# The transfers of a modulation matrix move from GpSimd's queue to ScalarE's queue, in groups of four

## What is computed

```
def adaln(cond, mod_w, mod_b):
    return jnp.split(jax.nn.silu(cond) @ mod_w + mod_b, 6, axis=-1)
```

## Time and profile before

| | before |
|---|---|
| median of three executions | 3646.84 us |
| the profiled execution | 3652.07 us |
| its span, first to last instruction | 3650.3 us |
| TensorE busy | 3305.8 us, 91% |
| mean granted TensorE clock | 0.947 |
| modulation tiles | 96 of 512 KB |

### The profile page before, as it was taken

One profiled execution on the slowest core, in us unless ns is written; L12 is line 12 of the kernel. 1 busy time (PEld: TensorE's weight loads), 2 busy tenths in 40 slices (PEclk: granted clock), 3 DMA queues, 4 the chain that ended last, 5 costly groups with the idle time before them and its releaser, 6 DMA issues.

```text
span 3650.3 us, 67685 instructions
## 1 busy us (share of the span) xinstructions
PE 3305.8 (91%) x25680; PEld 2864.8 (78%) x25680; DVE 2307.3 (63%) x4542; ACT 1387.8 (38%) x2128; POOL 380.0 (10%) x232
## 2 busy tenths in 40 slices
PE   7889899999998979889999999696779998899798
PEld 6678898989886859888999988473558877695798
DVE  5549786868975548976777895447632234636444
ACT  4334334343444333434344344323422223424343
POOL 1137500000000216810000000000000000000000
PEclk9789999999999979999999999897889999899899
DMA  7544445454454733445455445120012322211253
GB/s 252 173 138 141 143 136 188 148 188 148 151 172 161 271 127 126 151 142 177 156 171 168 147 154 190 35 76 1 1 57 93 98 97 90 79 53 47 93 183 124
DMA packets 131695, 478.62 MB, mean 131 GB/s; under 512 B 14512, under 2 KB 16560, under 8 KB 130992
## 3 DMA queue, kind: packets, MB, share of 16 engines
q1 hardware_dynamic: 115696, 416.72, 34.6%
q0 software_dynamic: 15808, 59.25, 4.8%
HBM read 474.87 MB, written 1.05 MB: 130 GB/s over the span
## 4 chain that ended last, share of the span: by engine, by line
PE 77%; DVE 18%; ACT 2%; issue 2%; DMA 1%; POOL 0%; SPq 0%; ACTq 0%; DVEq 0%
PE bank L448 76%; DVE arena L1478 1%; DVE arena L1677 1%; DVE arena L1475 1%; DVE arena L1522 1%; DVE arena L1474 1%; DVE arena L1477 1%; DVE arena L1501 1%; DVE arena L1476 1%; DVE Wl L1296 1%; DVE arena L1519 1%; PE bank L725 1%; DMA HA<-mods 1%; ACT Wh L911 1%; DVE arena L1664 1%
## 5 line engine op out<-in xcount | busy, mean ns | idle before, releaser
L448 PE MATMUL bank<-HR,Wh 128*128 128x256 f32 (+1 forms) x8192 | 1283.6, 310 | 142.1 <-DVE HR L1672 60.0
L1296 DVE TENSOR_TENSOR Wl<-ring,Wh 128x1024 fp32r<-128x1024 f32 x676 | 826.8, 1224 | 924.5 <-ACT Wh L911 923.4
L448 PEld LDWEIGHTS bank<-HR,Wh 128*128 128x128 f32 x8192 | 1137.9, 195 | 223.3 <-issue 69.1
L911 ACT CAST Wh<-ring 128x1024 fp32r<-128x1024 f32 x788 | 824.4, 1046 | 718.3 <-PE bank L448 715.1
L448 PE MATMUL bank<-Wh,HR 128*128 128x512 f32 (+1 forms) x3072 | 688.3, 354 | 2.7 <-DVE HR L1582 2.7
L448 PE MATMUL bank<-HR,Wl 128*128 128x256 f32 (+1 forms) x4096 | 659.0, 304 | 13.8 <-DVE Wl L1296 7.5
L448 PEld LDWEIGHTS bank<-HR,Wl 128*128 128x128 f32 x4096 | 577.0, 193 | 44.8 <-DVE Wl L1296 7.9
L448 PEld LDWEIGHTS bank<-Wh,HR 128*128 128x128 f32 x3072 | 535.1, 189 | 84.1 <-issue 4.2
L448 PE MATMUL bank<-Wl,HR 128*128 128x512 f32 (+1 forms) x1536 | 414.5, 351 | 0.0
L448 PE MATMUL bank<-arena 128*128 128x32 bf16 (+4 forms) x6624 | 342.4, 199 | 49.5 <-DVE arena L1566 11.3
L448 PEld LDWEIGHTS bank<-arena 128*128 128x128 bf16 (+3 forms) x6624 | 243.9, 105 | 109.6 <-issue 55.4
(11 more groups left out here) (224 smaller groups left out, 1931.0 us busy)
## 6 DMA issues: line engine op xcount, KB each, us to landing
ring<-weights SPq DMA_DIRECT2D x788, 512.0 KB, 3.3
HA<-mods POOLq DMA_DIRECT2D x96, 512.0 KB, 6.6
arena<-bias POOLq DMA_DIRECT2D x16, 256.0 KB, 2.9
arena<-keys POOLq DMA_DIRECT2D x2, 1024.0 KB, 5.4
HA<-mla POOLq DMA_DIRECT2D x1, 1536.0 KB, 6.5
K<-constants SPq DMA_DIRECT2D x1, 1402.0 KB, 6.4
X<-x SPq DMA_DIRECT2D x1, 1024.0 KB, 9.0
X<-context POOLq DMA_DIRECT2D x1, 1024.0 KB, 6.6
```

The costliest lines, as they stand in the source:

```text
L448: return nc.tensor.matmul(out, lhsT, rhs, start=first, stop=last)
L911: nc.scalar.copy(Wh[:, i % SPL], ring[:, i % RAW]).then_inc(S("hi_done"), 1)
L1296: v.tensor_tensor(Wl[:, i % SPL], ring[:, i % RAW], Wh[:, i % SPL], ALU.subtract).then_inc(S("lo_done"), 1)
```

## The change

POOL issues no modulation tile any more. ACT does, in groups of four: a function `mod_load(l, b)` issues the four tiles of one block. The first group stands ahead of the first norm of layer 0. The group of block b + 1 stands inside `mod_evac(l, b)`, behind its wait for the four products of block b and ahead of the copy. The first group of layer 1 stands behind ACT's two copies of the accumulator at the end of layer 0.

```diff
+            def mod_load(l, b):
+
+                for n in range(4 * (MODB * l + b), 4 * (MODB * l + b + 1)):
+                    act.dma_start(mslot[n % MSLOT], mod_d[n].rearrange("p (a b) -> p a b", a=4)).then_inc(S(f"mod_in{n % MSLOT}"), 16)
+
             def mod_evac(l, b):
 
                 act.wait_ge(S("mod_mm"), 4 * (MODB * l + b + 1))
+                if b + 1 < MODB:
+                    mod_load(l, b + 1)
                 after(act, S("mod_tp"), MODB * l + b - 1)
                 nc.scalar.copy(mstage[b % 2], macc(b)[:, :].rearrange("p (a b) -> p a b", a=2)).then_inc(S("mod_ev"), 1)
 
             for _i in range(2):
                 nc.scalar.copy(col[:, 90 + _i:91 + _i], eps[:, :]).then_inc(S("h_ev"), 1)
+            act.wait_ge(S("x_in"), 16)
+            mod_load(0, 0)
             for l in range(L):
...
                     nc.scalar.copy(acc[:, half, 0, :], bank[4 + half][:, :]).then_inc(S("acc_first"), 1)
+                if l + 1 < L:
+                    mod_load(l + 1, 0)
             norm_act("fin", X[:, :, XS], T, [(S("peer_out"), L)])
...
-            pool.wait_ge(S("const_in"), 16)
-            pool.wait_ge(S("x_in"), 16)
             for l in range(L):
-                after(pool, S("acc_done"), l)
-                for j in range(4 * MODB):
-                    n = 4 * MODB * l + j
-                    after(pool, S("mod_mm"), n - MSLOT + 1)
-                    pool.dma_start(mslot[n % MSLOT], mod_d[n].rearrange("p (a b) -> p a b", a=4)).then_inc(S(f"mod_in{n % MSLOT}"), 16)
                 pool.wait_ge(S("h_out"), SPLITS[f"m{l}"][1])
```

## The result

The changed kernel takes 3749.01 us (median of four runs, 3748.03 to 3750.19) against 3647.01 us (four runs, 3646.60 to 3647.25), a ratio of 1.028 with a 95% interval of 1.0262 to 1.0298. That is 102 us slower. The forecast was 3665 us with a range up to 3685.

What follows compares the result with a forecast made beforehand. PE was taken to bound the kernel, with 77% of the chain. Start 2.6, blocks 2 to 5 8.4, block 7 1.4 and head loop 6.1 summed to +18.5 us on 3646.84, 3665 us, range 3649 to 3685.

Steps and rivals of the forecast that it cites:

- H = 2.6 us: On ACT: issuing a group of four tiles holds everything behind it for 2.6 us, with ends 1.3 and 4.4.
- Start, +2.6: Ahead of layer 0's first norm square: the first group's whole hold is on the path, +2.6 us.
- Blocks 2 to 5, +4.2: In the projections: groups leave some 4.3 us later and tiles land late, +4.2 us per layer, +8.4 in two.
- the high end: Blocks 2 to 5: one ring tile ahead of each group's last, 1.4 us more each, together 6.5 us per layer.
- The middle, 4.2: Blocks 2 to 5: 4.2 us per layer, taken between the low end 1.8 and the high end 6.5.
- Cost nothing: Projections: ACT's late casts and evacuations have three tiles of lead, about 8.6 us of PE work, so cost nothing.
- Rival C: Blocks 2 to 5: new waits drop PE's clock, about 2.6 us more behind each block, eight times; 3686 us, chance 0.12.
- Block 7, +0.7: Behind block 7: the copy is held 2.6 us, less 1.9 gained on tile waits, +0.7 us per layer.
- Head loop, +3.1: Copies of blocks 8 and 9: holds delay head copies by 1.1 and 1.95 us, +3.1 per layer.
- Free parts: Block 10's copy and layer 1's first group: ACT's idle 5.9 and 2.94 us cover the holds; block 11 issues none.
- Rivals A: Whole kernel: issues are cheap but loads are still late, +4.6 us, 3651 us, chance 0.17.
- Rival B: Block 7: faster landing on the hardware queue removes all 10.3 us of waiting, about 3637 us, chance 0.06.

Runs made afterwards that it cites:

- run 4: The kernel before, POOL's transfers, with ACT held about 2.6 us by 11 tiny copies wherever the changed kernel issues a group ahead of a copy, and at the start: 3668.92 us.
- run 8: The kernel before, with block 6 multiplied behind the second of the last four projection tiles and copied behind the third's evacuation: 3648.40 us, ratio 1.0.
- Runs 1: The changed kernel, with ACT issuing block 5's group right behind block 4's products, one projection tile earlier: 3702.53 us, 1.0171 of before.
- run 2: The kernel before, POOL's queue, with only block 5's group delayed to about where the changed kernel issues it: 3701.72 us, 1.0149 of before.
- run 3: The changed kernel, with 16 unused matmuls of 512 columns ahead of the last four projection tiles: 3741.93 us, 1.0257 of before.
- run 6: The kernel before, POOL's queue, with the groups of blocks 2 to 5 delayed to about the changed kernel's moment: 3740.77 us, 1.0258 of before.
- run 5: The changed kernel, with ACT issuing the groups of blocks 2 to 5 right behind the products of the block in front: 3675.21 us, 1.0092 of before.
- run 7: The changed kernel, with groups 2 to 5 early, other groups behind their copies and the first behind the first square: 3663.51 us, 1.008 of before.
- run 9: The kernel before, POOL's queue, block 5's group late, and PE doing block 5 behind projection tile 14, not 15: 3677.09 us, 1.0065 of before.

## Why the prediction was wrong

The sign was right, the size was not: +18.5 forecast, +102 measured. The profiled executions differ by 96 us (3748.03 against 3652.07). Layer 0 can be laid beside the steps; layer 1's first square comes at 1198.18 instead of 1150.56, 47.6 us later in all.

- **H = 2.6 us, right.** Four issues take 2.59 us. The value was reached by a queue that takes in two and stalls; the trace shows 0.55 for the first and about 0.67 for each other, so the working was not what happens, only its sum. Nor was x worked off when the issue behind it ended at 3.80 us: the page of before has x landed 9.0 us behind its issue at 1.20. The Trainium skill's "usually small" (DMA: Bandwidth & Descriptors, "Issuing engines are not separate DMA queues") agrees with 0.65 us for an issue against 6.5 us to landing; what it costs depends on what waits behind it, and the holds alone cost 20 us in run 4.
- **Start, +2.6, right in size by luck.** The square starts 1.4 us later, not 2.6, since the issues begin beside the last cast; the first norm's sums then took 6.61 us for 5.42, and block 0 is 2.6 us late.
- **Blocks 2 to 5, +4.2, the first step that failed.** They end 18.9 us late, 16.3 behind the start's 2.6. The term's step was "the fourth lands 7.5 us behind the first issue". In the changed kernel the fourth landed 10.7, 11.4, 10.8 and 12.2 us behind it in these blocks. Below, block 5's group before (issues at 90.8 to 93.1) and after (108.8 to 110.8):

```profile
L1834 POOL DMA_DIRECT2D HA<-mods x4: 751/751/751, 90.8 to 93.1; - x4
...
DMA to landing us min/median/max: 3.9/6.3/8.8
```
```profile
L929 ACTq DMA_DIRECT2D HA<-mods x4: 547/652/653, 108.8 to 110.8; - x4
...
DMA to landing us min/median/max: 5.3/7.2/10.3
```

  The first fence is the kernel before, and this could have been read there: the last landed 11.0 us behind the first issue, and in blocks 2 to 4 it was 11.5, 12.7 and 11.2. Landing did not get slower; the time allowed for it shrank. POOL's groups had left 10.5 to 13.1 us ahead of their block, and PE takes the fourth some 1.5 us into it, so all but block 3's (0.70 us) were in time; ACT's left 6.3, 6.3, 8.1 and 6.4 us ahead. Even the high end, with one weight tile in between and so 8.9 us, was low for every group. By the prediction's own terms, two weight tiles in between give 3.3 + 5 x 1.4 = 10.3 us, an estimate that leaves 0.4 to 1.9 us open. The middle, 4.2, is shown by no run: the weight tile issued at 63.69, behind all four of block 2's group, landed at 70.67, ahead of the group's last at 71.69. The waits make 10.3 of the 16.3; the other 6 are products at half clock, in the blocks and behind them, and the 0.64 us that 8 products take behind a wait for 0.48 in a run of 32.
- **"Cost nothing" behind block 5, the step that broke the forecast.** The four tiles behind it were given no term, and with the turn they cost 20.4 us in each layer, 41 in all. The clock was in the prediction as Rival C, at a chance of 0.12 and for one tile behind each block, and "stretches between blocks run at 0.50" was among its own signs of being wrong. Rival C's condition, waits of 1 to 2 us, came true, and its place in three of the four blocks; its price of 2.6 us per block did not. Behind blocks 2 and 3 stand 256-column tiles, and the clock was back within the first of them, which took 4.5 and 4.4 us for 3.0. Behind block 5 stand the only four of 128 columns, and there it stayed down until they ended. The row of 43 us was not to be seen before; that those tiles differ in shape was. The Trainium skill (TensorE: Matmul & The Clock Gate, "The HAM clock gate") says the clock follows how busy PE has been, and gives sustained work as what brings it up. No run agrees for this stretch: PE was busy for 42.7 us of 42.7 at 0.50.
- **Block 7, +0.7, low.** The stretch from block 6's start to the sums of the attention grew by 3.3 us. The hold ahead of block 7's copy is there as described, 2.6 us. Block 6 ran at half clock, 3.41 us for 1.93. And the gain of 1.9 came out at 0.8 (10.5 us from block 6's end to block 7's, for 11.2): PE waited for tiles only 0.96 us where it had waited 5.14, but 3.35 us for block 6's copy, held by the same issues, where it had waited 0.70, and the group's last tile landed 9.3 us behind the first issue, not 7.5.
- **Head loop, +3.1, near.** From those sums to the end of the head loop it is 4.4 us. At block 9 PE waits 2.64 us for the copy L1016 where it had waited 0.57, 2.1 more for the 1.95 worked out. ACT's copies at L1016 (L1007 before) stand behind the groups as said:

```profile
221.60 2.78 ACTq L929 DMA_DIRECT2D HA<-mods  x4
224.42 0.59 ACT L937 COPY X<-bank 128x512 f32<-128x512 f32 x1 [4.14 <-issue]
224.90 0.48 ACT L1016 COPY arena<-bank 128x384 f32<-128x384 f32 x1
```

- **Free parts, right.** The idle time ahead of the first square of layer 1 is still 2.94 us, and the cast behind block 10 still had 5.64 us of idleness ahead of it.
- **Rivals A and B fell**: A with H, B by the landing time, 6.5 us for a tile and 10.7 to 12.2 for a group; run 8 adds that its prize would not have been paid in full. In Rival B's sum, 5H - 1.3 at H = 0.3 is 0.2 us and not 0.3, which changes nothing.

In layer 0 the steps read 2.6, 16.3, 20.4, 3.3 and 4.4, together 47.0 us. Runs 1, 2 and 3 show the clock as the cause of the largest one, runs 4 and 6 the shares of hold and lateness. The sign was right by the holds and the later issue, both in the forecast; that a loss of this size was missed is down to the landing time and the clock. What stays open is the rest of a group's landing time, and what makes the clock fall in one block and not in another. That each 4 KB row travels in 1 KB packets on ACT's queue was seen, but POOL's groups took as long, so it is not shown to matter.

## What to carry to other kernels

A transfer that leaves as soon as its slot is free should not be tied to a point in another engine's program, however near that point seems. Read from the trace of before how long a whole group takes to land and how far ahead of its use it leaves: here 11.0 to 12.7 us against 10.5 to 13.1, so 4 to 6 us of delay was more than the slack. Price a new wait on TensorE not by its length but by what runs behind it: here some 4 us of waits ahead of a long stretch of 128-column products cost 20 us more. And on an engine that others wait for, put issues behind the instruction they wait for, not ahead of it; from run 5 to run 7 that, with the first group behind its square, gave 12 us.

## What the runs showed of the hardware

In layer 0 the clock went down in or behind blocks whose waits added up to 2.77 us (block 2), 2.95 (block 3) and 4.21 (block 5) in the changed kernel and 4.18 in run 2, and stayed up with 1.02 (block 4) and with a single wait of 2.12 us (run 5). The sum alone does not decide it: in run 6 block 4's waits added up to 3.26 us and the clock stayed at 1.00. Once down, it stayed at 0.50 through 41.2 us of unbroken products of 128 columns (the changed kernel, runs 2 and 6). With 16 products of 512 columns (run 3) or one tile of 256-column products (run 9) ahead of them it was back at 1.00, and it stayed there through the same 128-column products.

Four issues of 512-piece tiles hold ACT for 2.59 us, with the engine itself idle. A tile on ACT's hardware queue lands no sooner (6.5 us) than on POOL's (6.6 us) when four are asked for at once, and a group of four beside the weight stream takes 10.7 to 12.2 us on ACT's queue and 11.0 to 12.7 us on POOL's to land (blocks 2 to 5 of layer 0, after and before).
